# Intake of a two-layer streaming encoder: the token tiles are requested around the first conditioning block, and the small products of that block move behind the first transposes

## What is computed

```
def ada_mod(c, w, b):
    return jax.nn.silu(c) @ w + b

def modulate(x, g, shift, scale):
    return rms_norm(x, g) * (1 + scale[:, None, :]) + shift[:, None, :]

def retention_layer(x, c, pos, r0, norm_g, ada_w, ada_b, w_in, gn_g, w_out):
    shift, scale, gate = jnp.split(ada_mod(c, ada_w, ada_b), 3, axis=-1)
    h = modulate(x, norm_g, shift, scale)
    q, k, v, g = jnp.split(h @ w_in, [RET_QK_W, 2 * RET_QK_W, 2 * RET_QK_W + RET_VW], axis=-1)
    ...
```

## Time and profile before

| | |
|---|---|
| time, median of 3 runs | 1715.49 us (1714.2 to 1717.23) |
| the profiled execution, its own time | 1713.18 us |
| its span, first to last instruction | 1711.4 us |
| PE busy | 1660.6 us, 97% of the span |
| DVE, ACT, POOL busy | 812.5, 611.8, 381.6 us |
| granted TensorE clock | 1.00 in every slice |

### The profile page before, as it was taken

The page is one execution under the profiler, slowest core; times in us unless marked ns, Lnnn a source line. Parts: engine busy times, 40 slices in busy tenths (PEclk is TensorE's granted clock), DMA queues, the critical chain, the costliest instruction groups (busy, mean ns, idle before and its releaser), DMA issues.

```text
span 1711.4 us, 22076 instructions
## 1 busy us (share of the span) xinstructions
PE 1660.6 (97%) x8377; PEld 1324.4 (77%) x8377; DVE 812.5 (47%) x1661; ACT 611.8 (36%) x999; POOL 381.6 (22%) x501
## 2 busy tenths in 40 slices
PE   5999999999999999999999999999999998999998
PEld 3999998777876766667668888888788886788887
DVE  4654442212245455546543333665554015777774
ACT  4311121111134434444440223623322116566673
POOL 2111112111233334333322123414211010111000
PEclk9999999999999999999999999999999999999999
DMA  9544545563456767577673312231323625555541
GB/s 314 200 154 163 184 145 203 173 222 127 166 174 202 242 184 239 184 222 245 198 243 118 111 37 78 107 105 60 103 83 101 209 99 154 179 175 167 170 139 59
DMA packets 145338, 275.40 MB, mean 161 GB/s; under 512 B 18099, under 2 KB 64335, under 8 KB 145234
## 3 DMA queue, kind: packets, MB, share of 16 engines
q1 hardware_dynamic: 112450, 181.92, 33.6%
q0 software_dynamic: 32784, 92.08, 15.9%
HBM read 193.51 MB, written 80.43 MB: 160 GB/s over the span
## 4 chain that ended last, share of the span: by engine, by line
PE 82%; DVE 6%; ACT 4%; issue 3%; DMA 2%; POOL 1%; SPq 0%; DVEq 0%; POOLq 0%; ACTq 0%
PE trunk_ps L1179 29%; PE in_ps_o L548 12%; PE in_ps_o L544 11%; PE trunk_ps L1174 5%; PE tail_ps L2146 5%; PE tail_ps L2137 3%; PE trunk_ps L1222 3%; PE trunk_ps L1206 3%; PE tail_ps L2097 2%; PE tail_ps L2110 2%; DVE room L1619 1%; PE in_ps_o L569 1%; PE trunk_ps L1217 1%; POOL room L1489 1%; PE trunk_ps L1282 1%
## 5 line engine op out<-in xcount | busy, mean ns | idle before, releaser
L1179 PE MATMUL trunk_ps<-w_hi,hT_hi 128*128 128x512 f32 x880 | 360.2, 409 | 0.6 <-DVE w_lo L210 0.6
L1179 PE MATMUL trunk_ps<-w_hi,hT_lo 128*128 128x512 f32 x880 | 349.0, 397 | 0.0
L1179 PE MATMUL trunk_ps<-w_lo,hT_hi 128*128 128x512 f32 x880 | 347.1, 394 | 0.0
L1179 PEld LDWEIGHTS trunk_ps<-w_hi,hT_hi 128*128 128x128 f32 x880 | 165.3, 188 | 54.9 <-issue 17.5
L1179 PEld LDWEIGHTS trunk_ps<-w_lo,hT_hi 128*128 128x128 f32 x880 | 165.4, 188 | 42.9 <-issue 5.0
L1179 PEld LDWEIGHTS trunk_ps<-w_hi,hT_lo 128*128 128x128 f32 x880 | 165.2, 188 | 39.4
L210 DVE TENSOR_TENSOR w_lo<-w_raw,w_hi 128x1024 fp32r<-128x1024 f32 x76 | 96.6, 1272 | 114.6 <-ACT w_hi L198 109.4
L544 PE MATMUL in_ps_o<-hT_hi,w_hi 128*128 128x384 f32 x384 | 130.5, 340 | 0.4 <-DVE hT_lo L698 0.4
L544 PE MATMUL in_ps_o<-hT_hi,w_lo 128*128 128x384 f32 x384 | 129.1, 336 | 0.0
L544 PE MATMUL in_ps_o<-hT_lo,w_hi 128*128 128x384 f32 x384 | 129.0, 336 | 0.0
L548 PE MATMUL in_ps_o<-w_hi,hT_hi 128*128 128x512 f32 x288 | 114.4, 397 | 0.0
(11 more groups left out here) (281 smaller groups left out, 3287.6 us busy)
## 6 DMA issues: line engine op xcount, KB each, us to landing
w_raw<-in_a_w_in SPq DMA_DIRECT2D x96, 256.0 KB, 3.4
room<-in_state_ret SPq DMA_DIRECT2D x64, 256.0 KB, 4.1
out_state_sample<-room POOLq DMA_DIRECT2D x64, 256.0 KB, 6.9
room<-in_b_ada_w SPq DMA_DIRECT2D x24, 512.0 KB, 6.5
scratch_qkT<-room POOLq DMA_DIRECT2D x48, 192.0 KB, 2.2
scratch_v_hi<-room POOLq DMA_DIRECT2D x36, 256.0 KB, 2.6
scratch_v_lo<-room POOLq DMA_DIRECT2D x36, 256.0 KB, 3.1
scratch_o<-room POOLq DMA_DIRECT2D x36, 256.0 KB, 3.3
```

Of the source, the lines that this page charges most:

```text
L1179: ins = pe.matmul(ps[:, bank, :], h[:, k, t * P:(t + 1) * P], w[:, (C0 + j) % 2, k, :], start=k + m == 0, stop=k == KT - 1 and m == 2)
```

## The change

On SP, the four transfers of block 0 are requested after tiles 0 to 5 of `x` instead of first of all; tiles 6 to 8 follow them. On DVE, groups 0 and 1 are both normed and scaled before the rows of block 0, group 2 after the modulation of block 0, and the low parts of slices 0 and 1 both come before the rows of block 1. On PE, `turn_group(0, 0)` and `turn_group(0, 1)` come before `ada(0)` and its fold, `turn(2)` before `ada(1)`, and the fold of block 1 stands between the second and third tile of slice 0's products instead of behind the fourth. Semaphore counts are renumbered to match. ACT's and POOL's programs are as before.

```diff
-        meant, inverted, scaled_of = ([(prepared, n + i) for n in (5, 11, 16)] for i in (0, 1, 4))
-        rows_out, mods_out = [(prepared, n) for n in (4, 21, 23, 25)], [(prepared, n) for n in (10, 22, 24, 26)]
+        meant, inverted, scaled_of = ([(prepared, n + i) for n in (4, 9, 16)] for i in (0, 1, 4))
+        rows_out, mods_out = [(prepared, n) for n in (14, 21, 23, 25)], [(prepared, n) for n in (15, 22, 24, 26)]
...
             chunks = weights + [after]
-            ada_block(0)
             sp.wait_ge(*c_cleared)
...
             for t in range(TILES):
+                if t == 6:
+                    ada_block(0)
                 sp.dma_start(xv[:, t], x_rows(t)).then_inc(rows_landed[t], ROWS)
...
             pe.wait_ge(*cT_ready)
+            turn_group(0, 0)
+            turn_group(0, 1)
             ada(0)
             fold_rows(0)
-            turn_group(0, 0)
-            turn_group(0, 1)
             pe.wait_ge(*squared[2])
             turn_group(1, 0)
             turn_group(1, 1)
             turn_group(0, 2)
             turn_group(1, 2)
+            turn(2)
             ada(1)
-            turn(2)
-            step(0)
-            fold_rows(1)
+            pe.wait_ge(h_ready, 1)
+            pe.wait_ge(pr.raw_split, 3)
+            for t in range(AHEAD):
+                if t == 2:
+                    fold_rows(1)
+                products(0, t, 0)
             step(1)
...
+            for g in range(2):
+                mean_squares(g)
+                scaled_rows(g)
             rows(0)
-            mean_squares(0)
-            scaled_rows(0)
             mods(0)
-            mean_squares(1)
-            scaled_rows(1)
             mean_squares(2)
+            scaled_rows(2)
             dve.wait_ge(turned, 1)
             dve.wait_ge(*mods_out[0])
             prompt_part(0, 0, 1)
-            scaled_rows(2)
...
                 if m == 0:
                     low(0)
+                    low(1)
                 if m < 3:
                     rows(m + 1)
-                low(2 * m + 1)
+                if m:
+                    low(2 * m + 1)
```

## The result

The changed kernel took 1723.73 us (median of 7 runs, 1719.05 to 1728.06) against 1715.49. The ratio is 1.0048, with an interval of 1.0031 to 1.0065: slower by 0.5%. The forecast was 1722.5 us, range 1718 to 1726. The profiled execution is the median one: 1723.73 us with a span of 1721.9, against 1713.18 and 1711.4.

A forecast was written before the change was run, and what follows sets the result against it. The prediction took the start of PE's unbroken run, behind a transfer-bound opening, as the bound. Tile 6 at 21.9 plus a 16.2 us chain put the first product 7.2 us late; less 0.2, +7.0 gave 1722.5 us, range 1718 to 1726.

The forecast's parts named there:

- Tile 6 at 21.9 (21.0 to 22.8): Landing of tile 6 of `x`, before at 19.8, with the stream 2.15 us late; bounds by how much of 1.8 returns.
- the 23.0: Landing of tile 6 if the skill's limit of about 358 GB/s held; the time would be 1.1 us above the sum.
- The chain behind it: Nine successive terms across ACT, DVE and PE from tile 6 to slice 0 modulated: 16.16 us, ending at 38.1.
- Terms 1 and 2: ACT's squares of tile 6 to inverse of root 1, 1.27 us; then inverse and scaling of three tiles to PE, 2.34.
- PE's clock: Open price in PE's opening work: slow level assumed; all fast 5.2 us less, a late rise about 2.1 us more.
- rival "fast level": PE runs the chain at its fast clock level: +1.8 us, 1717.3; chance 0.08 for (nearly) all of it.
- The later part: PE around slice 0's products: moved fold costs nothing of its own, gap before `turn(3)` closes, 0.20 us less.
- The covers: Items costed at nothing: POOL's first split ends 5 us ahead of the first product; block 2 there by 44, wanted at 49.9.
- The sum: Opening up to slice 0's products: first product 7.2 us late, less 0.2, +7.0 us; 1722.5 us on the median.
- The rival that tile 6 overtakes block 0: Tiles 6 to 8 slip past block 0 in the transfers, so ACT is not held: 1716.9 us; chance 0.06.
- A: The time at which tile 6 of `x` lands in the changed kernel, about 21.9 us, bounds 21.0 and 22.8.
- The rival of a gain: Slice 0 modulated earlier than 30.55 in the opening: at best 3.0 us faster, 1712.5; chance 0.03.

The follow-up runs named there:

- Experiment 3: The changed kernel with SP's requests back in the old order (block 0 first), the new orders on PE and DVE kept: 1721.99 us, ratio 1.0032.
- Experiment 1: The changed kernel with ACT taking the root of group 1 right after the squares of tile 5, not of tile 6: 1717.5 us, ratio 1.0010.
- experiments 9 and 10: The changed kernel with tiles 0 and 1 requested ahead of the cleared-buffer wait: 1721.22 us; the same plus group 1's root before tile 6's squares: 1715.53 us.
- experiment 6: The changed kernel with group 1's root earlier, tiles 0 and 1 requested before the wait, group 2 scaled before block 0's gains: 1715.2 us, ratio 0.9995.

## Why the prediction was right

It named the place, and the wait, the path and most terms of its sum were met. Two were not, and that they nearly cancel is luck. Against its own steps:

- **Tile 6 at 21.9 (21.0 to 22.8).** It came at 23.15, beyond the range, and this is the term that was mis-sized. The start of the stream was right (first tile issued at 3.67 against 3.8), but nothing was given back for the small transfers that no longer interrupt it. Of the 1.8 us that the prediction read as lost between 8 and 14, 1.2 are lost in the change as well (324 GB/s against 408), where no small transfer of SP runs any more. By 22 us the change had moved 1.12 + 1.94 + 2.90 = 5.97 MB; the kernel before 2.03 + 1.71 + 3.26 = 7.00, with 339 GB/s from 2 to 8. The 1.0 MB are 2.9 us at 351 GB/s, close to the whole delay of the issue. The Trainium skill ("DMA: Bandwidth & Descriptors", section "Where 436 GB/s comes from") has about 358 GB/s as the limit that binds here. The trace does not agree: in the change a stretch with block 0 and tiles mixed moved 363, tiles alone before it 408. So the delay is not that limit's, although the 23.0 that the prediction worked out from it lies nearest to the measured 23.15.
- **The chain behind it.** Terms 1 and 2 were 1.28 and 2.34, as said; the transposes took 0.84 (said 0.69); `rows(0)` until the fold 0.75; the gains 0.36; mean squares to inverse 0.43; the scaling 2.35; `modulated(0)` 1.25. With the faster terms below, the chain took 14.3 us instead of 16.2.
- **PE's clock** was named as the open price and changed twice. `ada(0)` until DVE took 3.04 instead of 3.78 and the fold 1.08 instead of 1.92, and the last transposes until DVE 0.58 instead of 0.94, together 1.9 us less; then `turn(2)` and `ada(1)` took 5.68 instead of 5.33. It is the rival "fast level" to about a third. The gain of 1.9 and the loss of 1.25 at tile 6 cancel for the most part, and the prediction foresaw neither's size: slice 0 at 37.5 (said 38.1), first product at 43.18 (said 43.4).
- **The later part** brought 0.38 us between first product and tables (29.98 against 30.36), said 0.2. The covers held: the first split on POOL ended at 38.0, block 2 was in time.
- **The sum**, +7.0 us, against 6.57 and 6.78 in the openings of the two profiles, counted from the first profile of before (5.1 and 5.3 from the second), and 7.2 and 8.2 us by the two ratios. The sum speaks of the opening alone; the rest of the time is what the experiments left open.

Beside these two terms a reason was wrong. The prediction laid the whole chain to block 0's 2 MB between tiles 5 and 6. Experiment 3 shows the chain without them, at some 5.5 us by the time. Experiment 1 shows that one root moved by one tile takes 4.9 us out of it, given the new requests, and experiments 9 and 10 that 2.0 to 2.9 us are the late stream's own. The rival that tile 6 overtakes block 0 did not occur: ACT waited 5.53 us for it. (That rival's bound was also misread: with slice 0 at 32.5 by its own sum, block 0 would decide from A below 32.5 - 16.2 = 16.3, not 14.9.) The rival of a gain fell as argued; experiment 6 shows that even with the loss mended there is nothing above the measurement.

## What to carry to other kernels

When transfers are reordered, look for instructions that were placed by the old order of arrival: a small one that stands behind a big one on its engine (here a root of 0.2 us behind the squares of the next tile) costs little while both arrive together, and up to the whole distance when they no longer do; here it was 4.9 us. Read the new order as a chain through all the engines before counting what comes earlier; here six tiles were squared 3.7 to 5.0 us earlier and nothing that ended last used it. And where transfers fill the opening, look for a wait ahead of the first of them; here taking two tiles out from behind it gave back 2.0 to 2.9 us of the 2.9 that the first request had come later.

## What the runs showed of the hardware

- The clock of PE in this opening is not a property of the program alone. In the two profiles of the kernel before, the first fold took 1.92 and 1.08 us and `turn(2)` 2.01 and 1.20; in the two of the change, the 16 records of `ada(0)` took 2.89 and 3.15 (and 3.64 in experiment 1). In the change it was at 1.2 GHz (0.50 granted) from 38 to 42, while PE was busy for all of the 4 us, after work with gaps; later drops, as the one near 494 (0.60), went with 1.2 to 1.9 us each.
- The same kernel's first transfers differ from execution to execution: silu at 11.09, 13.51 and, with the same requests in experiment 3, 12.55 us. The opening of the kernel before ended at 66.59 and 68.11. A difference of 1.5 us between the openings of two single profiles means nothing here.
- SP needed 6.95 us to issue the four transfers of block 0 behind six tiles, where they took 2.09 at the head of the queue; tile 6 was issued at 13.87 for that reason, and yet the transfers ran without a pause (share 1.02 to 1.08).
